# A mixed attention and mLSTM layer on one Trainium2 core: attention's queries, keys and gate computed channel by token

## The reference, cut to what matters

```python
h = rmsnorm(x, norm_g)
(a_q, a_k, a_v, a_z, i_q, i_k, i_w, b_q, b_k, b_v, b_z, b_o, b_i, b_f, g_a, g_b) = split(h @ w_in)
q_a, k_a = partial_rope(a_q), partial_rope(a_k)      # 8 heads of 64; the first 16 of each rotate
o_a = dsa_attention(q_a, k_a, a_v, q_i, k_i, w_i)    # softmax over the 128 best keys of each query
y_a = (o_a * silu(a_z)) @ w_branch_a
cell = mlstm(silu(conv(b_q, b_k)), b_v, gates(b_i, b_f))   # 4 heads of 128
y_b = (head_norm(sigmoid(b_o) * cell) * silu(b_z)) @ w_branch_b
x = x + (sigmoid(g_a) * y_a + sigmoid(g_b) * y_b) @ w_out
return rmsnorm(x, final_norm_g)
```

## Time and profile before

| | |
|---|---|
| median of 3 runs | 505.14 us (505.14 to 505.3) |
| the profiled execution | 505.35 us |
| its span in the trace | 503.6 us |
| TensorE's granted clock, mean | 0.998 |
| bytes moved by DMA | 48.94 MB |

### The profile page before, as it was taken

One profiled execution on the slowest core, in us unless ns is written; L12 is line 12 of the kernel. 1 busy time (PEld: TensorE's weight loads), 2 busy tenths in 40 slices (PEclk: granted clock), 3 DMA queues, 4 the chain that ended last, 5 costly groups with the idle time before them and its releaser, 6 DMA issues.

```text
span 503.6 us, 6823 instructions
## 1 busy us (share of the span) xinstructions
PE 494.5 (98%) x2518; PEld 411.6 (82%) x2518; DVE 261.4 (52%) x575; ACT 239.2 (47%) x434; POOL 213.0 (42%) x130
## 2 busy tenths in 40 slices
PE   8999999999999999999999999999999999999995
PEld 7688888888888888888788888888888888887885
DVE  3865777877899936525655567531111011125433
ACT  6757655555554455536568652413330333152322
POOL 0675131333344444247487451246534663373000
PEclk9999999999999999999999999999999999999999
DMA  8654432212343243112223112043234426453111
GB/s 284 188 153 128 126 87 79 84 48 80 83 111 99 85 117 104 52 43 85 57 70 85 43 43 65 20 125 104 62 87 125 126 58 193 126 149 144 42 55 72
DMA packets 44841, 48.94 MB, mean 97 GB/s; under 512 B 4996, under 2 KB 30212, under 8 KB 44808
## 3 DMA queue, kind: packets, MB, share of 16 engines
q1 hardware_dynamic: 43944, 47.65, 32.3%
q10 hardware_dynamic: 864, 0.86, 0.5%
HBM read 46.40 MB, written 2.11 MB: 96 GB/s over the span
## 4 chain that ended last, share of the span: by engine, by line
PE 94%; DMA 2%; SPq 1%; POOL 1%; ACT 1%; DVE 1%; issue 1%; DVEq 0%
PE pj L1486 24%; PE pj L1487 24%; PE pj L1488 24%; DMA w_raw<-in_w_in 2%; PE ob L1617 2%; PE tr L1606 2%; PE qb L1554 2%; PE qb L1553 2%; PE ob L1487 1%; PE qb L1487 1%; PE ob L1488 1%; PE qb L1488 1%; PE ob L1486 1%; PE qb L1486 1%; PE tr L1541 1%; PE qb L1601 1%
## 5 line engine op out<-in xcount | busy, mean ns | idle before, releaser
L529 POOL TENSOR_TENSOR w_lo<-w_raw,w_hi 128x1024 fp32r<-128x1024 f32 x70 | 168.9, 2424 | 156.3 <-ACT w_hi L875 156.0
L1486 PE MATMUL pj<-w_hi,h_hi 128*128 128x512 f32 x272 | 109.6, 403 | 0.0
L1488 PE MATMUL pj<-w_hi,h_lo 128*128 128x512 f32 x272 | 106.5, 392 | 0.0
L1487 PE MATMUL pj<-w_lo,h_hi 128*128 128x512 f32 x272 | 106.4, 391 | 0.0
L1486 PE MATMUL pj<-h_hi,w_hi 128*128 128x512 f32 (+1 forms) x200 | 78.1, 390 | 1.0 <-DVE h_lo L1129 1.0
L875 ACT ACTIVATE w_hi<-w_raw 128x1024 fp32r<-128x1024 f32 (+1 forms) x72 | 73.5, 1045 | 9.8 <-DMA w_raw<-in_w_out 6.3
L1488 PE MATMUL pj<-h_hi,w_lo 128*128 128x512 f32 (+1 forms) x200 | 77.9, 389 | 0.0
L1487 PE MATMUL pj<-h_lo,w_hi 128*128 128x512 f32 (+1 forms) x200 | 77.8, 389 | 0.0
L1488 PEld LDWEIGHTS pj<-w_hi,h_lo 128*128 128x128 f32 x272 | 51.1, 188 | 11.4
L1486 PEld LDWEIGHTS pj<-w_hi,h_hi 128*128 128x128 f32 x272 | 51.2, 188 | 8.3 <-issue 0.2
L1487 PEld LDWEIGHTS pj<-w_lo,h_hi 128*128 128x128 f32 x272 | 51.3, 188 | 8.0
(11 more groups left out here) (216 smaller groups left out, 817.3 us busy)
## 6 DMA issues: line engine op xcount, KB each, us to landing
w_raw<-in_w_in SPq DMA_DIRECT2D x60, 512.0 KB, 3.6
w_raw<-in_w_out SPq DMA_DIRECT2D x5, 512.0 KB, 3.5
x_tok<-in_x SPq DMA_DIRECT2D x4, 512.0 KB, 5.3
w_raw<-in_w_branch_a SPq DMA_DIRECT2D x8, 256.0 KB, 2.9
w_raw<-in_w_branch_b SPq DMA_DIRECT2D x8, 256.0 KB, 3.3
x_again<-in_x SPq DMA_DIRECT2D x1, 2048.0 KB, 9.3
w_late<-in_w_out SPq DMA_DIRECT2D x3, 512.0 KB, 6.1
out<-y_norm SPq DMA_DIRECT2D x4, 320.0 KB, 2.3
```

Source lines behind the costliest of these rows:

```text
L529: eng.tensor_tensor(lo[:, 0:m], raw_slot(n)[:, 0:m], hi[:, 0:m].bitcast(F32), ALU.subtract).then_inc(lo_by_dve if n in DVE_SLOTS else lo_b ...
L1486: pe.matmul(bank, a_hi, b_hi, start=first, stop=False)
L1487: pe.matmul(bank, a_hi, b_lo, start=False, stop=False)
L1488: return pe.matmul(bank, a_lo, b_hi, start=False, stop=last)
```

## The change

- Units of aq, ak and az are computed with the weights stationary, channels by tokens, as bq and bk were. Their transposes are gone from TensorE (stage_chan for aq and ak, out_a_chan).
- The rotation then mixes partitions. ScalarE copies a unit's bank to q_raw or k_raw; when all four units of a group are there, four DMAs of its own queue copy the rotated rows, eight partitions each and 64 KB, into each other's places in "swapped", which is zero elsewhere. VectorE multiplies the unit by cos_t, GpSimd multiplies swapped by sin_t and adds (jobs "turn"). cos_t and sin_t are 128 x 512 tables, 1 and 0 where nothing rotates; ScalarE fills 16 rows of each half in gate_rows from one bank, in which the table's rows are transposed along with the gates' rows.
- Keys are split in jobs "parts", at places 81, 88, 95 and 102, now from SBUF, where before they were split after each unit of ak, at places 50 to 62.
- gate_rows is one job of four transposes of 128 columns, gate_cols four of 64 columns. GpSimd clears gate_l, two_rows, cos_t, sin_t and swapped at the start.
- In attention each head has a job scale_a on VectorE, first at the next head's place: wait for the exponential, reciprocal of the sum, multiply the probabilities in SBUF. TensorE's transposes wait for it. The multiply of the gate by p_rec is gone.
- az is multiplied into o_at by channel blocks (gate_a) at places 12 to 15 of az and after it, rounded and split in rest_a. After the last unit ScalarE does its rest_a jobs behind the rounding of three slots and before the first sigmoid.

The core of the diff; left out are semaphores, waits for banks, addresses, and renamed rows.

```diff
+TURNED = ("aq", "ak")
...
-STAGED = [u for u in UNITS if u[0] in ("iq0", "iq1", "aq", "ak")]
+STAGED = [u for u in UNITS if u[0] in ("iq0", "iq1")]
+TURNS = [(g, b) for g in TURNED for b in range(KW)]
...
-    put(first["iq0"] + 8, "gate_rows", 1)
-    put(first["iq0"] + 8, "gate_rows", 0)
+    put(first["iq0"] + 8, "gate_rows")
     put(first["iq1"] + 3, "gate_cols")
     for n, u in enumerate(STAGED):
         put(4 * UNIT[u] + 4 + 2, "stage_chan", n)
+    for k in range(4):
+        put(first["ak"] + k, "swap", k)
+        put(first["ak"] + 8 + 3 * 7 + k, "swap", KW + k)
+    for m in range(len(TURNS)):
+        p = first["ak"] + 6 + 7 * m
+        put(p, "turn", m)
+        if TURNS[m][0] == "ak":
+            put(p + 3, "parts", m - KW)
...
+        if 1 <= p <= len(ATTN):
+            put(q, "scale_a", p - 1)
...
+    put(first["az"] + 12, "gate_a", 0)
+    put(first["az"] + 13, "gate_a", 1)
+    put(first["az"] + 14, "rest_a", 0)
+    put(first["az"] + 15, "gate_a", 2)
+    put(first["az"] + 15, "rest_a", 1)
...
+LAST_SIDE = (("gate_a", 3), ("rest_a", 2), ("rest_a", 3))
...
+        gate_l = at("gate_l", [P, TILES, P], F32, z_norm_b)
+        cos_t = at("cos_t", [P, SEQ], F32, z_a + 14336)
+        sin_t = at("sin_t", [P, SEQ], F32, z_a + 16384)
+        swapped = at("swapped", [P, KW, SEQ], F32, z_d)
+        raw_chan = [at("q_raw", [P, KW, SEQ], F32, z_g2), at("k_raw", [P, KW, SEQ], F32, z_a)]
+        k_chan = at("k_chan", [P, KW, SEQ], F32, z_g2)
...
+            pool.memset(gate_l[:, :, :], 0.0)
+            pool.memset(two_rows[:, :], 0.0)
+            pool.memset(cos_t[:, :], 1.0)
+            pool.memset(sin_t[:, :], 0.0)
+            pool.memset(swapped[:, :, :], 0.0).then_inc(blank_made, 1)
...
+                    if job[0] == "turn":
+                        m = job[1]
+                        g, b = TURNS[m]
+                        pool.wait_ge(rope_made, 4)
+                        pool.wait_ge(swap_in, 64 * (TURNED.index(g) + 1))
+                        pool.tensor_tensor(swapped[:, b, :], swapped[:, b, :], sin_t[:, :], ALU.mult).then_inc(sin_made, 1)
+                        pool.wait_ge(sin_made, m + 1)
+                        pool.wait_ge(cos_made, m + 1)
+                        part = swapped[:, b, :].rearrange("p (t n) -> p t n", n=P)
+                        pool.tensor_tensor(turned_rows(g, b), turned_rows(g, b), part, ALU.add).then_inc(turned, 1)
...
+                elif kind == "gate_rows":
+
+                    act.wait_ge(blank_made, 1)
                     wait_full(act, job)
-                    act.activation(q_a[:, j, :, :],
-                                   bank_of(job)[:, :].rearrange("p (b t) -> p b t", t=P), ACT.Copy)\
-                        .then_inc(q_a_turned, 1)
+                    for first, dst in ((64, cos_t), (96, sin_t)):
+                        for rows in (slice(0, ROT), slice(A_DIM, A_DIM + ROT)):
+                            act.activation(dst[rows, :], bank_of(job)[first:first + ROT, :], ACT.Copy)\
+                                .then_inc(rope_made, 1)
+                elif kind == "swap":
+
+                    n, k = divmod(job[1], 4)
+                    act.wait_ge(unit_out, UNIT[(TURNED[n], KW - 1)] + 1)
+                    if n:
+                        act.wait_ge(turned, KW * n)
+                    e, half = divmod(k, 2)
+                    to, src = A_DIM * e + HALF * half, A_DIM * e + HALF * (1 - half)
+                    act.dma_start(swapped[to:to + HALF, :, :], raw_chan[n][src:src + HALF, :, :]).then_inc(swap_in, 16)
+                elif kind == "parts":
+                    b = job[1]
+                    if b == 0:
+                        act.wait_ge(gate_tok_made, 1)
+                    act.wait_ge(turned, KW + b + 1)
+                    for e in range(2):
+                        src, hi, _ = k_part(b, e)
+                        act.activation(hi, src, ACT.Copy).then_inc(k_hi_made, 1)
...
+                elif g in TURNED:
+                    act.activation(raw_chan[TURNED.index(g)][:, j, :], src[:, :], ACT.Copy).then_inc(done, 1)
...
+                elif kind == "parts":
+                    b = job[1]
+                    for e in range(2):
+                        src, hi, lo = k_part(b, e)
+                        dve.wait_ge(k_hi_made, 2 * b + e + 1)
+                        dve.tensor_tensor(lo, src, hi.bitcast(F32), ALU.subtract).then_inc(k_lo_made, 1)
...
-                        s = i * A_HEADS
-                        dve.wait_ge(probs_made, s + A_HEADS)
-                        link(dve.reciprocal(p_rec[:, s:s + A_HEADS], p_sum[:, s:s + A_HEADS]))
...
+                elif kind == "scale_a":
+                    s = job[1]
+                    w = (ATTN[s][0] + 1) * P
+                    dve.wait_ge(probs_made, s + 1)
+                    link(dve.reciprocal(p_rec[:, s:s + 1], p_sum[:, s:s + 1]))
+                    dve.tensor_scalar(probs[:, s % 2, 0:w], probs[:, s % 2, 0:w], p_rec[:, s:s + 1], None, ALU.mult)\
+                        .then_inc(probs_scaled, 1)
+                elif kind == "gate_a":
+                    b = job[1]
+                    dve.wait_ge(zt_made, TILES + b + 1)
+                    dve.wait_ge(o_at_made, TILES)
+                    gate = gate_a[:, (b + 2) % KW, :].rearrange("p (i t) -> p i t", t=P)
+                    dve.scalar_tensor_tensor(out=o_at[:, :, b, :], in0=gate, scalar=0.5, in1=o_at[:, :, b, :],
+                                             op0=ALU.mult, op1=ALU.mult).then_inc(oa_gated, 1)
+                elif kind == "rest_a":
+                    b = job[1]
+                    dve.wait_ge(oa_gated, b + 1)
+                    dve.wait_ge(o_hi, TILES + b + 1)
+                    oa = oa_lo[:, b, :].rearrange("p (i t) -> p i t", t=P)
+                    dve.tensor_tensor(oa, o_at[:, :, b, :],
+                                      oa_hi[:, b, :].rearrange("p (i t) -> p i t", t=P).bitcast(F32), ALU.subtract)\
+                        .then_inc(o_lo, 1)
...
+                if g in TURNED:
+                    if g == "ak" and j == 0:
+                        dve.wait_ge(swap_in, 64)
+                    if (g, j) == ("aq", 0):
+                        dve.wait_ge(rope_made, 4)
+                    dve.wait_ge(unit_out, u + 1)
+                    dve.tensor_tensor(turned_rows(g, j), pj[u % 2][:, :].rearrange("p (t n) -> p t n", n=P),
+                                      cos_t[:, :].rearrange("p (t n) -> p t n", n=P), ALU.mult).then_inc(cos_made, 1)
...
-                elif g == "az":
-                    ring = gated[:, (TILES + j) % 2, :]
-                    dve.wait_ge(zt_made, TILES + j + 1)
-                    heads = ring.rearrange("p (h d) -> p h d", d=A_DIM)
-                    rec = p_rec[:, j * A_HEADS:(j + 1) * A_HEADS]
-                    dve.tensor_tensor(heads, heads, rec.unsqueeze(2).to_broadcast([P, A_HEADS, A_DIM]), ALU.mult)\
-                        .then_inc(gated_a_made, 1)
...
+                    for j in range(TILES):
+                        ins = pe.transpose(bank[:, j * ROWS:(j + 1) * ROWS], two_rows[:, j * P:(j + 1) * P],
...
-                    pe.wait_ge(probs_made, s + 1)
+                    pe.wait_ge(probs_scaled, s + 1)
...
-                elif kind in ("out_a_chan", "out_b_chan"):
-                    pe.wait_ge(gated_a_made if kind == "out_a_chan" else gated_b_made, job[1] + 1)
-                    ring = gated[:, OUT_ORDER.index(job) % 2, :]
...
-                        if g in CHAN_GROUPS:
+                        if g in CHAN_GROUPS + TURNED + ("az",):
...
-                    if c == 0 and s == 0:
-                        side(LAST_SIDE)
```

More of the change, by code:

```diff
@@ L163 @@
 SHARE = 640
-OA_LO_AT = {first_quarter("az") + 4 * j + 8: j for j in range(TILES - 2)}
-LAST_SIDE = ("out_a_chan", TILES - 1)
+LAST_SIDE = (("gate_a", 3), ("rest_a", 2), ("rest_a", 3))
 RING_OF = {"small_tok": "tr", "ik_chan": "tr", "gate_rows": "tr", "gate_cols": "tr", "stage_chan": "tr",
-           "probs_chan": "tr", "out_a_chan": "tr", "out_b_chan": "tr",
+           "probs_chan": "tr", "out_b_chan": "tr",
            "score": "q", "qk_b": "q", "qk_a": "q", "pv_b": "o", "pv_a": "o", "kt_b": "tr", "state_b": "o"}
-NOT_PE = ("scales_in", "scales", "decay_b")
+NOT_PE = ("scale_a", "gate_a", "rest_a", "scales_in", "scales", "decay_b", "swap", "turn", "parts")
 def fills():
@@ L178, in fills @@
     bank, before, order = {}, {}, {}
-    for job in [job for p in sorted(SIDE) for job in SIDE[p] if job[0] not in NOT_PE] + [LAST_SIDE]:
+    for job in [job for p in sorted(SIDE) for job in SIDE[p] if job[0] not in NOT_PE]:
         order[job] = len(order)
@@ L193 @@
 BANK, BEFORE, ORDER = fills()
-OUT_ORDER = sorted([("out_a_chan", j) for j in range(TILES)] + [("out_b_chan", j) for j in range(TILES)],
-                   key=ORDER.get)
+LAST_PV = ("pv_a", len(ATTN) // QUAD - 1)
 ROUNDS = TOPK // 8
@@ L421, in hybrid_kernel @@
         en_made = sem("en_made")
```

(28 more changed lines are left out.)

153 lines of the change are left out of this document (68 added, 85 removed).

## The result

The changed kernel takes **529.29 us** (median of 4 runs, 528.62 to 530.37) where the kernel before takes 505.14: 1.048 times as long, 95% interval 1.046 to 1.050. The forecast was 517.4, in 503.5 to 523. Slower was right; the size was half of what came. The profiled execution took 528.62 us, its span 526.7, 23.1 more than before.

The account below looks back on a forecast made before the run. TensorE, busy 494.5 of 503.6 us, was taken as the bound. The sum was 505.35 - 5.9 + 4.8 + 10.1 + 3.3 = 517.6, less 0.2: 517.4 us, range 503.5 to 523.

Parts of the forecast that it names:

- transposes and other work gone: On TensorE: 12 sets of transposes gone, fewer for the gates' rows and columns; together -5.9 us.
- conv 7 late: Before attention: two key-split jobs on full VectorE delay the last of eight convolutions, which TensorE awaits; +3.3 us.
- the loop through the exponential: In attention: masked maximum, exponential, reciprocal, multiply and copy form one serial loop per head; +4.8 us, 2 to 7.
- the multiply beside GpSimd: In attention: VectorE's multiply of the probabilities waits till GpSimd's whole instruction is over; +10.1 us.
- all that was costed at nothing: Clears, swaps, turns, table copies, queries turned on VectorE and the end of az: covered by idle time, no cost.
- the rival in which the loop is hidden: In attention: TensorE runs ahead and VectorE is half idle, so only the transposes count; 499.2 us, chance 0.13.
- The path to conv 7: VectorE's work before attention, followed from conv 4: the last convolution ends 4.4 us later, 1.0 of it slack.
- The rival without the wait: In attention: the multiply does not wait for GpSimd; 505.5 us, from 503 to 507, chance 0.2.
- where it strikes: Ends of bz and az: GpSimd's gating and weight remainders hold multiplies, 12.0 us in all, +10.1 with gating starts half counted.
- none at 128 columns: Sign in attention: TensorE waits some 15 us for probs or probs_t from 250 us on, none at 128 columns.
- the three races with gating: Ends of bz1, bz2, bz3: GpSimd's gating and the multiply start within 0.05 us; +1.25 each, half counted.
- more is held up: Rival: az's end or GpSimd's remainders after its turns are late; 3 to 6 us over forecast, 520 to 523, chance 0.09.

Follow-up runs that it names:

- 499.57: The changed kernel without the division of the probabilities and with the four key splits at places 93, 97, 101 and 105: 499.57 us.
- 506.19: The changed kernel with scale_a left out, so the probabilities go on undivided: 506.19 us, ratio 1.0019.
- 510.19: The changed kernel with the multiply of the probabilities on ScalarE, the reciprocal staying on VectorE: 510.19 us.
- the late splits: The four parts jobs moved from places 81, 88, 95 and 102 to 93, 97, 101 and 105; alone on the changed kernel: 523.53 us.
- the filled wait: The changed kernel with 16 extra matmuls of 128x512 into an unused bank, just before TensorE waits for the last convolution: 526.70 us.

## Why the prediction was wrong

The runs form a ladder, and each step stands for one term of the sum:

| term | forecast | measured | by |
|---|---|---|---|
| transposes and other work gone | -5.9 | -5.6 | 505.2 to 499.57 |
| conv 7 late | +3.3 | +6.6 | 499.57 to 506.19 |
| the loop through the exponential | +4.8 | +4.0 | 506.19 to 510.19 |
| the multiply beside GpSimd | +10.1 | +19.1 (all that VectorE's multiply brings) | 510.19 to 529.29 |

This is one order of taking things away, and the steps are not independent: with the multiply on VectorE, moving it behind the copy alone brought 9.2 us back.

- **Right: the transposes, the loop, and all that was costed at nothing.** The loop's price is that of the chain over ScalarE, so it stands for the one on VectorE only roughly; the last term has the rest, such as the 3.5 us that went when the multiply was cut to 32 columns (529.29 to 525.79). The time of the rival in which the loop is hidden (499.2) came only without the division and with the late splits (499.57). The path to conv 7 was right as well: in the changed kernel it starts 4.7 us later than in that one (168.35 against 163.63), and 4.4 were forecast. Less 1.0 of slack that is 3.4, where the sum has 3.3.
- **Right in kind, too small: "the multiply stands still beside GpSimd".** The Trainium skill, "SBUF — State Buffer", section "Who interferes with whom", has the engine that comes second wait for the whole instruction of the first, and 2.40 us for 32 columns is just that. The rival without the wait (505.5) is out. The first step that failed is "where it strikes", the term of 10.1: the multiplies stood still for 14.1 us. I went through the ends of bz and az and gave the stretch before them 0.3 us. At 128 keys it struck three times, 2.45, 1.05 and 1.88 us, 4.5 over what they take alone; "none at 128 columns" was wrong, TensorE waited 2.8 us there. And the three races with gating, of which I counted half, were all lost (1.0, 1.1 and 1.0 us over). Two of the four that follow an end cost less than the 1.4 forecast for each, 0.2 and 1.0.
- **Missing altogether: what a wait does to TensorE's clock.** The sum took a wait as its own length. In the profile 6.4 us of the 23.1 are matmuls at 1.2 GHz behind a wait: 3.4 in attention, and 3.0 behind conv 7, where the wait itself was forecast at 3.3 and measured at 3.6. Behind conv 7 this is shown by the filled wait. In attention the 3.4 are a bound, as told there. With both in full the forecast is 523.8, and with the standing still as measured, 14.1 for 10.1, it is 527.8; some of that is counted too high, so the last few us to 529.29 stay open. The Trainium skill, "TensorE: Matmul & The Clock Gate", section "HAM oscillation — how this bites in real kernels", warns of waits that bring the clock down time after time; in this trace it was down after three of the five waits of 2.0 us or more. No row of before has TensorE at half clock but at its very end, and I took that for having no such cost.
- The chance of "more is held up" (0.09, at 520 to 523) was too low and its price as well, by the same omission.

## What to carry to other kernels

Before a VectorE instruction that reads and writes SBUF goes between two steps of TensorE, lay GpSimd's timeline beside it: what counts is not its width but how long the GpSimd instructions are that can stand beside it, and what is queued behind it (moving it behind the copy alone brought 9.2 us). ScalarE is the place for such a multiply if its queue has room, and short GpSimd instructions are the second choice. Where TensorE is the bound, a wait of some us is to be costed with the half-speed stretch that can follow it, and it can pay to fill it with work that nobody needs.

## What the runs showed of the hardware that was not expected

- Of two engines that start within 0.04 us of each other, either may get in first: the multiplies at 239.26 and 293.07 lost by it, the second though it is recorded 0.04 us ahead; chunk_w won at 169.36 and lost at 169.33. One such toss goes with some 5 us of a whole kernel's time (503.3 to 508.8).
- A multiply held up is shown from its issue on, so a row of 2.45 us says nothing of work: the same form takes 0.29 alone. Beside GpSimd's small instructions (root_t, 0.22) the excess was under 0.1.
- Which waits halve the clock is not their length alone: after 2.92 us at 295.2 and 2.0 at 309.4 it was halved for 3.4 us each, after one of 2.44 at 281.0 and one of 3.33 at 325.6 it was not. With the filled wait it was halved in another place (321.5 to 324.9). What decides it stays open.
